# Sample states in their working layout, new states in one place, expert rows by indirect transfer

## The reference, cut to what matters

```python
def step(S, inp):                       # S: the state, v x k, per sample and head
    sa = einsum('bhvk,bhk->bhv', S, -kk_t)
    S = S * w_t + sa x (kk_t * a_t) + v_t x k_t
    return S, einsum('bhvk,bhk->bhv', S, r_t)

logits = x @ w_router; top_val, top_idx = top_k(logits, 2); gate = softmax(top_val)
for e in range(8):                      # gate, up: 1024 x 2816, down: 2816 x 1024
    out += combine[..., e] * (silu(x @ w_gate[e]) * (x @ w_up[e])) @ w_down[e]
```

## Time and profile before

| | |
|---|---|
| median of 3 runs | 1506.03 us (1505.18 to 1509.32) |
| the profiled execution | 1507.48 us, span 1505.6 us |
| TensorE busy | 1445.3 us, 96% of the span |
| VectorE, ScalarE, POOL busy | 457.4, 218.0, 164.0 us |
| DMA | 384.88 MB, mean 256 GB/s |

### The profile page before, as it was taken

The page is one execution under the profiler, slowest core; times in us unless marked ns, Lnnn a source line. Parts: engine busy times, 40 slices in busy tenths (PEclk is TensorE's granted clock), DMA queues, the critical chain, the costliest instruction groups (busy, mean ns, idle before and its releaser), DMA issues.

```text
span 1505.6 us, 39356 instructions
## 1 busy us (share of the span) xinstructions
PE 1445.3 (96%) x17896; PEld 937.7 (62%) x17896; DVE 457.4 (30%) x987; ACT 218.0 (14%) x485; POOL 164.0 (11%) x207
## 2 busy tenths in 40 slices
PE   7988989999999999987999999999999999999997
PEld 5766877777777777776654545555454555545453
DVE  2399231111024558665331111112111011211123
ACT  3043220000003422233120000000000000000001
POOL 4147100000000325025100000000000000000100
PEclk9999999999999999998899999999999999999999
DMA  9444024343533420304569999999999999999995
GB/s 370 144 171 134 1 115 165 114 150 130 168 102 114 134 85 3 59 4 143 198 210 415 413 414 413 414 414 414 414 394 411 412 386 411 374 414 387 393 402 214
DMA packets 104400, 384.88 MB, mean 256 GB/s; under 512 B 29199, under 2 KB 31471, under 8 KB 104106
## 3 DMA queue, kind: packets, MB, share of 16 engines
q1 hardware_dynamic: 97200, 365.84, 62.7%
q0 software_dynamic: 3616, 12.85, 2.2%
q10 hardware_dynamic: 3418, 3.68, 0.7%
HBM read 375.59 MB, written 6.73 MB: 254 GB/s over the span
## 4 chain that ended last, share of the span: by engine, by line
PE 88%; DVE 8%; issue 1%; ACT 1%; DMA 1%; SPq 0%; DVEq 0%
PE bk L1619 30%; PE bk L1636 15%; PE bk L1100 12%; PE bk L785 9%; PE bk L1113 6%; PE bk L1541 2%; PE bk L1585 2%; PE bk L1015 2%; PE bk L1207 1%; DVE left L2200 1%; DVE tops L2198 1%; DMA ring<-in_weights 1%; PE bk L1128 1%; PE bk L1149 1%; DVE sc_p L2185 1%
## 5 line engine op out<-in xcount | busy, mean ns | idle before, releaser
L1619 PE MATMUL bk<-part,xe 128*32 128x352 f32 x6144 | 457.4, 459 | 0.3 <-DVE xe L2674 0.3
L1619 PEld LDWEIGHTS bk<-part,xe 128*32 128x32 f32 x6144 | 207.5, 110 | 244.9 <-issue 242.5
L1636 PE MATMUL bk<-part,hidT 128*32 128x256 f32 x4224 | 231.4, 379 | 1.2 <-DVE hidT L2713 1.2
L1636 PEld LDWEIGHTS bk<-part,hidT 128*32 128x32 f32 x4224 | 142.0, 110 | 88.5 <-issue 2.6
L2709 DVE TENSOR_TENSOR hp<-sg,bk 128x352 f32<-128x352 f32 x48 | 37.6, 783 | 467.2 <-PE bk L1619 467.2
L1100 PE MATMUL bk<-xn,ring 128*128 128x288 f32 x704 | 173.9, 411 | 2.7 <-DVE xn L2276 2.7
L1100 PEld LDWEIGHTS bk<-xn,ring 128*128 128x128 f32 x704 | 135.7, 193 | 40.6 <-issue 3.0
L785 PE MATMUL bk<-mx,ring 128*128 128x288 f32 x384 | 98.3, 416 | 0.0
L785 PE MATMUL bk<-xg,ring 128*128 128x288 f32 x336 | 88.0, 421 | 4.7 <-DMA ring<-in_weights 3.1
L785 PEld LDWEIGHTS bk<-mx,ring 128*128 128x128 f32 x384 | 73.4, 194 | 21.1 <-issue 0.8
L1113 PE MATMUL bk<-hid,ring 128*128 128x288 f32 x352 | 85.5, 406 | 0.0
(11 more groups left out here) (535 smaller groups left out, 1273.0 us busy)
## 6 DMA issues: line engine op xcount, KB each, us to landing
part<-in_moe_gate SPq DMA_DIRECT2D x136, 704.0 KB, 12.2
part<-in_moe_up SPq DMA_DIRECT2D x136, 704.0 KB, 14.0
part<-in_moe_down SPq DMA_DIRECT2D x128, 704.0 KB, 14.9
ring<-in_weights SPq DMA_DIRECT2D x121, 512.0 KB, 4.3
ro<-in_weights SPq DMA_DIRECT2D x8, 512.0 KB, 5.2
expert_rows<-ye ACTq DMA_DIRECT2D x7, 384.0 KB, 7.1
Sn<-in_state_wkv SPq DMA_DIRECT2D x8, 256.0 KB, 5.2
out_wkv_sample<-Ss SPq DMA_DIRECT2D x32, 64.0 KB, 2.2
```

The lines of the kernel that those rows point to most:

```text
L1619: last = mm(banks[g][32 * c:32 * c + 32, 0:FQ], xe[:, k, 32 * g:32 * g + 32], parts[ph % 3][:, FH * k + FQ * c:FH * k + FQ * c + FQ], star ...
L1636: last = mm(down_bk[g // 2][32 * q:32 * q + 32, 256 * (g % 2):256 * (g % 2) + 256], hidT[:, half, g, 32 * m:32 * m + 32], parts[ph % 3][:, ...
```

## The change

- The host lays the initial sample states out as `Ss` wants them, and one transfer of 16 KB per partition loads them. `Sn`, the four `old_state` groups and their copies go, and "E" and `BKm` no longer wait for them.
- `new_state` multiplies the other way round: 4 wide matmuls against the identity, 16 small ones for the outer products; the new state keeps k on the partitions. All eight are made before `turn_y`, and each is stored with one transfer of 256 KB. The host reorders the output.
- The expert loop: `gather` is used once, for expert 0, ahead of the loop. POOL scales the rows of all tokens by their RMS factor, stores them in DRAM (`token_rows`), and fetches the 96 rows of each further expert with an indirect transfer. The row numbers are made in expert 0: VectorE compares ranks with slot numbers (`slots_of`), TensorE multiplies by the token numbers (`token_of_slot`), VectorE takes the diagonal (`rows_of_slots`). VectorE turns the fetched rows in 12 small transposes (`rows_turned`).
- The phases are gate0, up0, gate1, up1, down0, down1, the buffers 2, 0, 1 in turn. SP loads 24 pieces without waiting for the number of blocks; the first 8 go to the buffer where the ring and `Ss` were, so that they wait until the states are stored.
- `y_prompt` is stored in 12 transfers, the first 128 rows in 8 of 128 columns.

```diff
@@ SP @@
-                for b in range(NB):
-                    sp.dma_start(Sn[half_(b % 2), b // 2].rearrange("p (h k) -> p h k", h=RH),
-                                 I["state_wkv"][0, b].rearrange("h v k -> v h k")).then_inc(sn_in, 16)
+                sp.dma_start(Ss[:], I["states"]).then_inc(sn_in, 16)
...
-        for hp in range(4):
-            new_state(hp)
-        sp.wait_ge(om_mm, KC + 2)
-        sp.wait_ge(out_done, 16 * (OUT_1 + 1))
+        for hp in range(KC):
+            turned_s(sp, f"K{hp}")
+            sp.dma_start(O["wkv_sample"][:, hp], Ss[:, hp]).then_inc(ws_out, 16)
+        for i in range(KC):
+            sp.wait_ge(slot_in[i], _sum[i])
+        sp.wait_ge(ws_out, 16 * KC)
...
-            if n == 5:
+            if n == KC:
+                sp.wait_ge(om_mm, KC + 2)
+                sp.wait_ge(out_done, 16 * (OUT_1 + 1))
+            if n == KC + 5:
                 sp.wait_ge(om_mm, KC + 4)
             piece_load(n)
-        for hp in range(4, KC):
-            new_state(hp)
-        sp.wait_ge(ws_out, 32 * RH)
-        sp.wait_ge(blocks_ok, 1)
...
-        for n in range(KC):
-            i, q = n // 4, n % 4
+        for n in range(KC + KC // 2):
+            i = n // KC
+            w_ = (P, 256)[i]
@@ TensorE @@
-        turned_s(pe, "K0")
-        new_state(3)
+        for hp in range(3, KC):
+            turned_s(pe, f"K{hp - 3}")
+            new_state(hp)
...
+        def token_of_slot(blk):
+            pe.wait_ge(in_slot_ok, blk + (IDX_OK + 1))
+            for i in range(3):
+                slots = in_slot[:, i].rearrange("p (e g s) -> p g e s", g=3, s=32)
+                for g in range(3):
+                    last = mm(down_bk[0][32 * g:32 * g + 32, 0:NE * 32], token_no[:, i], slots[:, g], start=i == 0, stop=i == 2)
+            last.then_inc(row_mm, 1)
...
             widen(blk, e, 0, gate_bk, gu_mm, gate0_k)
             widen(blk, e, 1, up_bk, up_mm, up0_k)
+            if e == 0:
+                token_of_slot(blk)
             widen(blk, e, 2, gate_bk, gu_mm, gate1_k)
+            widen(blk, e, 3, up_bk, up_mm, up1_k)
...
-            narrow(blk, e, 3, 0)
-            widen(blk, e, 4, up_bk, up_mm, up1_k)
+            narrow(blk, e, 4, 0)
@@ VectorE @@
+        def rows_turned(blk, e):
+            j = e % 2
+            dve.wait_ge(token_in[j], blk * (16 * (NE // 2)) + (K_IN + 16 * (e // 2 + 1)))
+            for q in range(4):
+                for g in range(3):
+                    row = xr[32 * g:32 * g + 32, j].rearrange("p (k q d) -> p q k d", k=KC, q=4)
+                    last = V.transpose(xe[32 * q:32 * q + 32, :, 32 * g:32 * g + 32], row[:, q])
+            last.then_inc(xe_ok, 1)
...
@@ POOL @@
+        pool.wait_ge(xe_mm, 1)
+        pool.wait_ge(gn_pool, gp_at["acc1"])
+        for i, (t0, tn) in enumerate(TILES):
+            last = G_.tensor_scalar(xr[0:tn, i], xr[0:tn, i], ssf[0:tn, i:i + 1], None, ALU.mult)
...
+        pool.dma_start(token_rows[0:TP].rearrange("(i p) d -> p i d", p=P), xr[:, 0:2]).then_inc(tokens_out, 16)
+        pool.dma_start(token_rows[TP:T], xr[0:NS, 2]).then_inc(tokens_out, 16)
+        pool.wait_ge(tokens_out, IK_IN + 32)
...
+            for e in range(NE):
+                if e >= 2:
+                    pool.wait_ge(xe_ok, blk * (2 * NE) + 2 * e - 1)
...
+                pool.indirect_dma_start(xr[0:CAP, e % 2], None, token_rows,
+                                        bass.IndirectOffsetOnAxis(ap=row_no[:, e:e + 1], axis=0)).then_inc(token_in[e % 2], 16)
```

More of the change, by code:

```diff
@@ L429, in build @@
     got = sbt("got", [P, 2, D], at=starts["xT"])
+    token_no = sbt("token_no", [P, 3, 32])
+    row_no = sbt("row_no", [CAP, NE], U32)
+    free_rows = sbt("free_rows", [P, NE * N_BLK])
+    row_no_f = sbt("row_no_f", [CAP, NE])
+    in_slot = sbt("in_slot", [P, 3, NE * CAP], at=starts["xT"])
+    assert ends["in_slot"] <= starts["ms"]
+    slot_no = sbt("slot_no", [P, P], at=starts["xT"])
+    slot_mine = sbt("slot_mine", [CAP, NE, 32], at=starts["pick"])
+    assert ends["slot_mine"] <= starts["xe"]
     assert ends["got"] <= starts["ms"]
@@ L548, in piece_in @@
         return (slot_in[i], _sum[i], 16) if part == 2 else (*pieces_in[KC // 2 * part + i // 2], 32)
-    PHASES = ("gate0", "up0", "gate1", "down0", "up1", "down1")
+    PHASES = ("gate0", "up0", "gate1", "up1", "down0", "down1")
+    PART_OF = (2, 0, 1) * 2
     USES_AT = [0]
@@ L1329, in _ @@
             last.then_inc(d_mm, 1)
-        def old_state(n):
-            pe.wait_ge(sn_in, 16 * NB)
-            turned_s(pe, f"S{n - 1}" if n else "B")
-            for hp in (2 * n, 2 * n + 1):
-                for b2 in range(NB // 2):
-                    last = nc.tensor.transpose(bk[6 + hp % 2][:, b2 * P:(b2 + 1) * P], Sn[:, b2, P * hp:P * hp + P], C["ident"])
-            last.then_inc(sm_mm, 1)
         for p2 in range(2):
@@ L1365, in _ @@
             last.then_inc(d_mm, 1)
-            old_state(2 + half)
         for hp in range(KC):
@@ L1469, in new_state @@
             pe.wait_ge(sm_pool, sp_at[f"d{hp}"])
+            for odd in range(2):
+                for par in range(2):
+                    r = half_(par)
+                    mm(bk[K_BANKS[hp][odd]][half_(par ^ odd), 0:HALF_NB], C["ident64"][r],
+                       Ss[r, hp].rearrange("p (j o v) -> p o j v", o=2, v=HD)[:, odd], start=True, stop=False,
+                       skip_group_check=True)
             for b in range(NB):
@@ L1473, in new_state @@
                     r = half_(par)
[L1474 to L1480 removed]
+                    last = mm(bk[K_BANKS[hp][odd]][half_(par ^ odd), at:at + HD], BKm[r, hp, b], Zs[r, hp],
                               start=False, stop=True, skip_group_check=True)
@@ L1695, in _ @@
                 scatter(blk, g)
-            gather()
     @block.scalar
@@ L2008, in _ @@
         new_state(2)
+        new_state(3)
         root(1)
-        new_state(3)
+        for hp in range(4, KC):
+            new_state(hp)
         for j, c in enumerate(ON_POOL):
@@ L2038, in _ @@
         last.then_inc(gx_ok, 1)
-        for hp in range(5, KC):
-            new_state(hp)
         gate_bk, down_bk = bk[0:3], bk[6:8]
@@ L2748, in _ @@
         V.scalar_tensor_tensor(blocks[:], blocks_f[0:1, 1:2], 1.0, blocks_f[0:1, 2:3], ALU.add, ALU.add).then_inc(blocks_ok, 1)
-        picks(0, 0).then_inc(pick_ok, 1)
+        picks().then_inc(pick_ok, 1)
+        link(V.tensor_tensor(slot_no[:], C["ident"], C["slots"], ALU.mult))
+        link(V.tensor_reduce(row_ss[:, 0, 0:1], slot_no[:], AX.X, ALU.add))
+        for i in range(3):
+            V.tensor_scalar(token_no[:, i], C["ones"][:, 0:32], row_ss[:, 0, 0:1], float(P * i), ALU.mult, ALU.add)
         for b in range(1, T // CAP):
@@ L2986, in laid_out, with states_of @@
     arrays["pairings"] = pairings()
+    states = np.asarray(inputs["state_wkv"])[0].reshape(NB, KC, 2, HD, HD)
+    arrays["states"] = np.ascontiguousarray(states.transpose(2, 4, 1, 0, 3).reshape(P, KC, NB * HD))
     arrays["consts"] = np.concatenate([CONSTS[k] for k in COL], 1)
     return arrays
+def states_of(a):
+    halves = a.reshape(2, HD, KC, 2, NB // 2, HD)
+    states = np.zeros((1, NB, RH, HD, HD), np.float32)
+    for par in range(2):
+        for odd in range(2):
+            states[0, odd::2, par::2] = halves[par ^ odd, :, :, odd].transpose(2, 1, 3, 0)
+    return states
 def kernel(**inputs):
```

162 lines of the change are left out of this document (83 added, 79 removed).

## The result

The changed kernel took 1491.6 us (median of 4 runs, 1490.39 to 1496.42); the kernel before, with one more run, 1506.37 us (1505.18 to 1509.32). The ratio is 0.9902, interval 0.9883 to 0.9922: faster by 1.0%. The forecast was 1481.0 with a range of 1473 to 1490: right in direction, 10.6 us too low, and the time lies just outside the range.

A forecast was written before the change was run, and what follows sets the result against it. TensorE was taken to bound the kernel (88% of the chain of waits), with the DMA next at a thin margin. The terms summed to -25.0 us, giving 1481.0 us as median, range 1473 to 1490.

The forecast's parts named there:

- DMA in the new loop: Expert loop: DMA needs 85.8 us an expert against 85.3, covered by 42 us of lead; no stall, cost 0.
- End: Stores of y_prompt: 12 transfers instead of 8, four more SP issues of 0.51 us, +2.1 us (ends 0.5 and 2.1).
- Rival D: Expert loop: the DMA becomes the bound; at 354 GB/s +55 us, 1536 us; chance 0.03.
- The load itself was hidden and stays so: Sample states' load, 8 transfers from 621 us, not used until 657: its time was hidden and stays hidden.
- Expert loop: gathers out and order: Expert loop: seven gathers removed -27.2 us, token_of_slot +1.3, up1 ahead of down0 in the last expert -1.7.
- rival B: Last expert: the earlier up1 waits 6.7 us for hidden half 0 behind the got additions; 1488 us, chance 0.15.
- C: Expert loop: fetched rows come late and the gather returns as a wait, 27 us back, 1508 us; chance 0.05.
- Sample states, load side: Ahead of the experts: TensorE's state transposes and the VectorE and ScalarE copies gone, -2.5 us (ends 0 and -4.3).
- Store side: New states before turn_y: +1.2 us of delay against clock regained by filling TensorE's idle time, -0.5 us (ends +1.2 and -2.5).
- the +1.0 taken: First gather at the logits: lower clock without states 4 and 5 ahead of it, +1.0 us (ends 0 and +2.6).
- the +1.5: Before gate0 of expert 0: TensorE idles where states 6 and 7 stood, lower clock, +1.5 us (ends 0 and +4).
- POOL beside VectorE: After the first gather: VectorE's gain multiplication meets POOL's scaling of the token rows, +1.0 us (ends 0 and +2.1).

The follow-up runs named there:

- experiment 2: Changed kernel with 32 bytes instead of 4 KB fetched per row by a direct transfer, rows of experts 1 to 7 left out: 1485.84 us, ratio 0.9862.
- experiment 1: Changed kernel without the 16 weight pieces loaded past the last expert, stores waiting for no later load: 1486.13 us, ratio 0.9874.
- Experiment 5: Changed kernel with the sample states loaded in eight transfers of 256 KB, spread behind TensorE's product groups over 32 us: 1488.41 us, ratio 0.9859.
- 6: Kernel before with only the state part of the change, expert rows still gathered by TensorE for each expert: 1510.58 us, ratio 1.0007.
- 9: Changed kernel with the states loaded in eight transfers of 256 KB, all issued one after the other: 1484.79 us, ratio 0.9853.
- 3: Changed kernel with each expert's 96 rows fetched by a direct transfer of consecutive rows, same bytes, choice of rows left out: 1495.09 us, ratio 0.992.
- 7: Changed kernel without loads past the last expert and with eight last stores of 256 columns that wait for no piece: 1483.47 us, ratio 0.9839.
- experiment 10: Changed kernel without loads past the last expert, with eight last stores and states in eight spread transfers: 1480.29 us, ratio 0.9837.

## Why the prediction was wrong, point by point

**The steps that failed are "DMA in the new loop" and "End".** The first put an expert's DMA work at 85.8 us, let 11 of the 42 us of lead go, and said "No stall: the cost is 0". In the loop TensorE did wait only 0.6 us, but that was luck: the forecast left 31 us of lead, and it was used up by then. SP's issue shows 87.7 and 88.9 us an expert in place of 85.8. Two sizes were off. A fetch of rows was taken at 1.2 us and costs 1.7 to 2.0 (experiment 2, and the rates). And the 414 GB/s of the kernel before do not come back: over two whole experts it is 409 here (1050.89 to 1226.34), and 411 in experiment 2, without the fetches, at a share of 1.02 both times. No run splits the rest. More than that, the sum counted 360 pieces that have to land, and SP loads 16 more, for which the stores of y wait. At 1.72 us a piece they are 27.5 us of issue behind the last real piece (1437.1), and the last is issued at 1464.9, 9 us ahead of the first store, with a landing time of 15 us and more. "End" then said "+2.1" for four more issues. It is +8.2, of which 6.6 go with the loads past the end (14.8 us from the first store to the end of the span, 8.1 in 1); the four issues themselves are the other 1.6. Rival D had this mechanism in the wrong place: it asked whether the DMA bounds the loop, not what stands behind the loop.

**"The load itself was hidden and stays so" failed too.** The landing was indeed hidden. The transfer's side effect was not: +1.9 us of stall, then 1.4 us (L1240's sixteen, 3.60 against 2.2 at full clock) and 0.7 (L1249's eight, 1.61 against 0.87), 4.0 of the +4.2 to T's first products. Experiment 5 takes it away, 6 brings it into the kernel before, 9 cuts the stall to 1.90 us. That TensorE lacks instructions in the stall, and that they come late because of the data, is what the packets of instructions show by their times; how the queues pass them on is not measured.

**Expert loop: gathers out and order** held: -26.3 against -27.6. token_of_slot took 1.2 us (1.3 forecast). The fetches landed in 9.2 us and never held anyone. The last expert ran without a gap but for the 0.6 us in front of down0; rival B did not occur, nor C.

**Sample states, load side:** -2.5 forecast for TensorE's transposes and the copies; the stretch from T's first product to F's shortened by 4.2 here (38.0 us before, 33.8 now, by the first starts). In the eleven traces with the new load it is 33.3 to 36.2 us, 35.0 in the mean, against 38.0 and 37.6 in the two without. Right on average, and the spread between executions is as large as the term.

**Store side** -0.3 against -0.5, which is right by size and not by mechanism. The idle stretch of TensorE in 710 to 714 is filled:

```profile
710.00:714.00 4.00, 3.84 (x133) 2.97 (x124) 3.21 (x6) 2.96 (x11) 1.32 (x1) 1.00 0.66 245
714.00:718.00 4.00, 3.27 (x19) 2.09 (x18) 2.48 (x6) 1.03 (x3) 1.77 (x2) 1.00 0.54 200
770.00:774.00 4.00, 4.00 (x47) 2.11 (x43) 3.15 (x29) 0.00 (x0) 0.00 (x0) 0.55 0.00 0
```

With new states in it, 714 to 718 kept its clock, but 720 to 724 had 0.70, and the first two projections took 9.35 us, as before. In experiments 1, 3, 6 and 7, with the same code in this place, they start later and run at full clock. In experiment 1:

```profile
721.17 7.85 PE bk L1539 x32
```

The one pays for the other: from T's first product to gate0 it is 118.3 to 118.5 us in the changed kernel and in experiments 1, 2, 3, 6 and 7, however F and the projection lie. The first gather, whose idle stretch was emptied, ran at 0.55: 6.59 us, +1.4 for the +1.0 taken. Behind gate0 the +1.5 did not come in this execution (28.61 us for 384 instructions at clock 1.00); in experiments 2 and 5 it did (30.10 and 30.30 us).

**POOL beside VectorE:** +1.0 forecast, 0 measured. Timelines of VectorE, then of POOL:

```profile
776.30 0.96 DVE L2664 TENSOR_TENSOR xe<-xe,vecT 128x768 f32<-128x768 f32 x1
```

```profile
775.22 10.08 POOL L2982 TENSOR_SCALAR xr<-xr,ssf 128x1024 f32<-128x1024 f32 x3 [9.19 <-PE bk L1584]
```

The multiplication took what it took before, in the middle of POOL's scaling. By the lock of the Trainium skill ("SBUF — State Buffer", Who interferes with whom) an operation of VectorE with two SBUF inputs should have waited for the whole of POOL's; the trace does not agree here. POOL's own three took 3.4 us each where I had 1; only the rows' way to DRAM stood behind them, and no engine waited for that.

The chance of 0.92 for faster held. The range failed because its upper end came from rivals inside the loop and the ends of the listed terms; a term that was not on the list had no width.

## What to carry to other kernels

When a bound engine gets faster, list everything that the second resource still has to do before the program may end, work that nobody needs included, and price it at the new rate: the loads past the end were free in the kernel before and cost 6.6 us of the span here. Look at landing times expert by expert: if they grow, the DMA is already behind, though no engine waits yet. In this kernel a large early load wants to be spread, even where its landing is hidden: the one transfer cost TensorE 4.8 us against the spread load, in the stall and in the clock after it. A term that does not change a stage's period can still reappear behind the stage's last instruction.

## What the hardware showed that I had not expected

- One transfer of 2 MB (8.6 us, up to 414 GB/s) went with a stall of 3.2 to 3.5 us in TensorE in each of the six kernels whose chain shows it; 1.90 with eight of 256 KB in a burst, 1.29 with eight whose issue took SP 8 us, 0.69 in experiment 10, where one of 256 KB goes out at a time.
- TensorE went on 2.3 to 2.8 us after a packet of the instruction queue, in ten kernels, and that packet came 3.0 to 3.3 us behind the same product with the one transfer of 2 MB, 0.6 to 0.9 with the old or the spread load.
- 96 rows of 4 KB cost a saturated DMA 1.7 to 2.0 us, about twice their bytes' share (0.95), chosen rows or consecutive ones. The busy share (1.00 to 1.04) says nothing of it; only the GB/s do.
- SP issued stores of 64 KB and of 128 KB at the same 0.47 us each (5.61 / 12 and 3.79 / 8).
- POOL's tensor_scalar of 128x1024 by a value per partition took about 3.4 us, its copy of the same size 1.04.
